# mLSTM stage: short denominator and norm, finished between the next head's products; values projected before queries and keys

## What is computed

```python
qk = silu(causal_depthwise_conv(qk_pre, conv_qk))
...
num = w_inter[..., None] * einsum('bhtd,bhde->bhte', qc, C) + einsum('bhts,bhse->bhte', qk, vc)
den = w_inter * einsum('bhtd,bhd->bht', qc, n) + sum(qk, axis=-1)
h = num / maximum(abs(den), exp(-m_t))[..., None]
...
h = rms_norm(h, head_norm.reshape(MLSTM_HEADS, 1, MLSTM_V_DIM))
h = merge_heads(h).astype(xn.dtype) * sigmoid(og)
```

## Time and profile before

| | |
|---|---|
| median of 3 runs | 2963.53 us (2962.91 to 2967.25) |
| the profiled execution | 2963.58 us |
| its span in the trace | 2961.7 us |
| mean granted TensorE clock | 0.934 of 2.4 GHz |
| TensorE (PE) busy | 2567.9 us, 87% |
| VectorE (DVE) busy | 1241.7 us, 42% |
| ScalarE (ACT) busy | 960.6 us, 32% |
| GpSimd (POOL) busy | 987.9 us, 33% |
| the heads of this stage | from 974.8 to 1236.5 us of the span |

### The profile page before, as it was taken

The page is one execution under the profiler, slowest core; times in us unless marked ns, Lnnn a source line. Parts: engine busy times, 40 slices in busy tenths (PEclk is TensorE's granted clock), DMA queues, the critical chain, the costliest instruction groups (busy, mean ns, idle before and its releaser), DMA issues. The chain is left out here.

```text
span 2961.7 us, 37204 instructions
## 1 busy us (share of the span) xinstructions
PE 2567.9 (87%) x14314; PEld 1852.1 (63%) x14314; DVE 1241.7 (42%) x1578; ACT 960.6 (32%) x1354; POOL 987.9 (33%) x469
## 2 busy tenths in 40 slices
PE   8998898799897899789879999869978698579996
PEld 5776676588775566568658877647577487223334
DVE  5443623566554533362256655341744513411112
ACT  4542422444323233243234442242422321211112
POOL 5222322344375311142233437523111333122321
PEclk9999999899999988899989999979999799799998
DMA  3111222122264111122112226412000121599992
GB/s 120 64 44 57 99 72 84 59 98 99 102 219 147 43 43 42 36 92 100 57 71 99 87 73 237 156 57 92 1 3 25 64 85 57 209 356 346 361 352 99
DMA packets 76275, 333.79 MB, mean 113 GB/s; under 512 B 17114, under 2 KB 21210, under 8 KB 51802
## 3 DMA queue, kind: packets, MB, share of 16 engines
q1 hardware_dynamic: 62336, 313.98, 29.3%
q0 software_dynamic: 13824, 18.19, 1.8%
HBM read 372.67 MB, written 16.78 MB: 131 GB/s over the span
## 5 line engine op out<-in xcount | busy, mean ns | idle before, releaser
L495 POOL TENSOR_TENSOR dense_w_lo<-weights,dense_w_hi 128x1024 fp32r<-128x1024 f32 x84 | 203.3, 2423 | 467.0 <-ACT dense_w_hi L486 467.0
L220 PE MATMUL bank<-dense_s_hi,dense_w_hi 128*128 128x512 f32 x672 | 270.2, 402 | 65.6 <-DVE dense_s_lo L456 35.5
L221 PE MATMUL bank<-dense_s_lo,dense_w_hi 128*128 128x512 f32 x672 | 266.5, 397 | 0.0
L222 PE MATMUL bank<-dense_s_hi,dense_w_lo 128*128 128x512 f32 x672 | 266.5, 397 | 0.0
L486 ACT ACTIVATE dense_w_hi<-weights 128x1024 fp32r<-128x1024 f32 x84 | 88.9, 1058 | 346.2 <-PE bank L222 319.5
L220 PEld LDWEIGHTS bank<-dense_s_hi,dense_w_hi 128*128 128x128 f32 x672 | 129.6, 193 | 104.8 <-POOL dense_w_lo L495 39.3
L1245 DVE TENSOR_TENSOR hidden<-up_y 128x512 f32 x44 | 158.2, 3596 | 64.6 <-ACT up_y L1208 64.0
L222 PE MATMUL bank<-xn_r,weights_r 128*128 128x512 f32 x448 | 177.7, 397 | 0.0
L220 PE MATMUL bank<-xn_r,mix_r 128*128 128x512 f32 x352 | 141.7, 403 | 38.0 <-DVEq L1233 38.0
L1586 DVE SCALAR_TENSOR_TENSOR xn<-mix,xn 128x1024 f32<-128x1024 f32 x64 | 122.3, 1911 | 119.6 <-DMA mix<-in_modulation 106.6
L2743 PE MATMUL bank<-moe_weights,mix 128*64 128x512 f32 x320 | 151.1, 625 | 17.4 <-DMA experts_more_up<-in_experts_up,moe_more_up 17.4
(11 more groups left out here) (634 smaller groups left out, 6134.8 us busy)
## 6 DMA issues: line engine op xcount, KB each, us to landing
weights<-in_w_up SPq DMA_DIRECT2D x44, 1024.0 KB, 4.9
moe_weights<-in_experts_up SPq DMA_DIRECT2D x40, 1024.0 KB
mix<-in_modulation SPq DMA_DIRECT2D x64, 512.0 KB, 4.5
weights<-in_w_xattn SPq DMA_DIRECT2D x24, 1024.0 KB, 5.0
weights<-in_experts_up SPq DMA_DIRECT2D x24, 1024.0 KB
weights<-in_w_down SPq DMA_DIRECT2D x44, 512.0 KB, 3.7
moe_weights<-in_experts_down SPq DMA_DIRECT2D x40, 512.0 KB
weights<-in_w_attn SPq DMA_DIRECT2D x8, 1536.0 KB, 6.3
```

The costliest lines, as they stand in the source:

```text
L220: nc.tensor.matmul(out, left.hi, right.hi, start=first, stop=False)
L221: nc.tensor.matmul(out, left.hi, right.lo, start=False, stop=False)
L222: return nc.tensor.matmul(out, left.lo, right.hi, start=False, stop=last)
L495: nc.gpsimd.tensor_tensor(w[b].lo[:, :], units.rows(b, 0, D, 0, D), w[b].hi[:, :], ALU.subtract).then_inc(w_split, 1)
```

## The change

The denominator is no longer summed into all 128 partitions over 512 columns. It is folded: block b of 128 positions goes into partitions 32b to 32b+31 of bank 6, over 128 columns, by a stationary tile of 32 columns of ones; the row exp(-m) goes into the next 128 columns of the bank in the same way. Absolute value, maximum and reciprocal then work on 128 x 128. Four products with one repeated column of the identity as the stationary tile widen it again to 128 x 512 in bank 7 (`widen`), and ScalarE copies that to `den`. The mean of squares is folded, rooted, inverted and widened in the same way; the scaling reads the widened norm from bank 7.

On TensorE this work no longer stands at the end of the head but between the products of the next one: `widen_den` after the first quarter of the value projection, `head_means` after the third quarter, `widen_head` after the query half of the query/key projection. The last head's three steps stand alone at the end. Values are now projected first, then queries and keys, then the gate, and ScalarE's rounding, GpSimd's rests and VectorE's copies follow that order. SyncE waits for the query/key projection (fourth count), then issues the loads of slots 0 and 1, then waits for the gate.

```diff
+        QK, VALUE, GATE = range(3)
+        ORDER = (VALUE, QK, GATE)
@@ -1277,7 +1281,7 @@
...
-        den = sb("den", [P, T])
+        den, den_short = sb("den", [P, T]), sb("den_short", [P, P])
@@ -1290,16 +1294,14 @@
...
-                for s in range(3):
-                    sp.wait_ge(proj_done, 6 * i - 6 + 2 * s + 2)
+                for s, last in ((QK, 4), (VALUE, 2), (GATE, 6)):
+                    sp.wait_ge(proj_done, 6 * i - 6 + last)
                     units.load(sp, i, s)
@@ -1311,40 +1313,71 @@
...
+            def widen(bank, short):
+                for b in range(TT):
+                    mm = nc.tensor.matmul(bank[:, b * P:(b + 1) * P], g.ident[:, 32 * b:32 * b + 1].broadcast_to([P, P]), short,
+                                          start=True, stop=True)
+                return mm
+
+            def widen_den(i):
+                pe.wait_ge(den_inverted, i + 1)
+                widen(g.bank[7], den_short[:, :]).then_inc(den_wide, 1)
+
+            def head_means(i):
+                for j in range(2):
+                    pe.wait_ge(squared, 2 * i + j + 1)
+                    for b in range(TT):
+                        mm = nc.tensor.matmul(g.bank[6][32 * b:32 * b + 32, 2 * P:3 * P], g.mean_256[:, 0:32],
+                                              sq[:, j, b * P:(b + 1) * P], start=(j == 0), stop=(j == 1))
+                mm.then_inc(mean_done, 1)
+
+            def widen_head(i):
+                pe.wait_ge(head_inverted, i + 1)
+                widen(g.bank[7], g.rstd[:, 0:P]).then_inc(head_wide, 1)
+
             def head(i, first):
-
-                pe.wait_ge(h_ready, 2 * i + 1)
-                for j in range(2):
-                    if j == 0:
-                        pe.wait_ge(w_split[0], i + 1)
-                    for k in range(KT):
-                        c = k * W + j * P
-                        mm = split_products(nc, g.bank[j][:, :], w[0].cut(c, c + P), norm.split[k], k == 0, k == KT - 1)
-                    mm.then_inc(proj_done, 1)
-                pe.wait_ge(w_split[1], i + 1)
-                pe.wait_ge(std_ready, i + 1)
+                pe.wait_ge(w_split[VALUE], i + 1)
+                if not first:
+                    pe.wait_ge(v_ready, 2 * i)
                 for t in range(TT):
                     for k in range(KT):
                         mm = split_products(nc, g.bank[2 + t // 2][:, t % 2 * VD:(t % 2 + 1) * VD], norm.split[k].cut(t * P, (t + 1) * P),
-                                            w[1].cut(k * W, k * W + VD), k == 0, k == KT - 1)
+                                            w[VALUE].cut(k * W, k * W + VD), k == 0, k == KT - 1)
                     if t % 2 == 1:
                         mm.then_inc(proj_done, 1)
+                    if not first:
+                        if t == 0:
+                            widen_den(i - 1)
+                        if t == 2:
+                            head_means(i - 1)
+                pe.wait_ge(w_split[QK], i + 1)
+                if not first:
+                    pe.wait_ge(h_ready, 2 * i)
+                for j in range(2):
+                    for k in range(KT):
+                        c = k * W + j * P
+                        mm = split_products(nc, g.bank[j][:, :], w[QK].cut(c, c + P), norm.split[k], k == 0, k == KT - 1)
+                    mm.then_inc(proj_done, 1)
+                    if not first and j == 0:
+                        widen_head(i - 1)
                 if first:
                     pe.wait_ge(G_ready, 1)
                     for t in range(TT):
                         mm = nc.tensor.transpose(g.bank[4][:, t * H:(t + 1) * H], G[:, t * P:(t + 1) * P], g.ident[0:H, 0:H])
                     mm.then_inc(G_turned, 1)
                     pe.wait_ge(Gc_ready, 1)
...
+                pe.wait_ge(w_split[GATE], i + 1)
...
+                        mm = split_products(nc, g.bank[4 + j][:, :], w[GATE].cut(c, c + P), norm.split[k], k == 0, k == KT - 1)
...
                 pe.wait_ge(qk_ready, 2 * i + 2)
                 pe.wait_ge(rows_ready, 2 * i + 2)
+                if not first:
+                    pe.wait_ge(head_scaled, 2 * i)
@@ -1358,21 +1391,25 @@
...
-                nc.tensor.matmul(g.bank[3][:, :], g.ones[0:H, :], rows[:, 1, :], start=True, stop=True)
                 for kb in range(TT):
                     pe.wait_ge(p_ready, 4 * i + kb + 2)
-                    for j in range(3):
-                        left = v[:, kb, j * P:(j + 1) * P] if j < 2 else g.ones[:, :]
-                        mm = nc.tensor.matmul(g.bank[j][:, kb * P:T], left, probs_T[:, kb, kb * P:T], start=(kb == 0),
-                                              stop=(kb == TT - 1), skip_group_check=True)
+                    for j in range(2):
+                        nc.tensor.matmul(g.bank[j][:, kb * P:T], v[:, kb, j * P:(j + 1) * P], probs_T[:, kb, kb * P:T], start=(kb == 0),
+                                         stop=(kb == TT - 1), skip_group_check=True)
+                for b in range(TT):
+                    nc.tensor.matmul(g.bank[6][32 * b:32 * b + 32, P:2 * P], g.ones[0:H, 0:32], rows[:, 1, b * P:(b + 1) * P],
+                                     start=True, stop=True)
+                for kb in range(TT):
+                    for b in range(kb, TT):
+                        mm = nc.tensor.matmul(g.bank[6][32 * b:32 * b + 32, 0:P], g.ones[:, 0:32], probs_T[:, kb, b * P:(b + 1) * P],
+                                              start=(kb == 0), stop=(kb == b), skip_group_check=True)
                 mm.then_inc(sums_done, 1)
-                for j in range(2):
-                    pe.wait_ge(squared, 2 * i + j + 1)
-                    mm = nc.tensor.matmul(g.bank[3][:, :], g.mean_256[:, :], sq[:, j, :], start=(j == 0), stop=(j == 1))
-                mm.then_inc(mean_done, 1)
             head(0, True)
             with pe.Fori(1, units.n) as i:
                 head(i, False)
+            widen_den(units.n - 1)
+            head_means(units.n - 1)
+            widen_head(units.n - 1)
 
...
 
...
                 for j in range(2):
-                    act.wait_ge(proj_done, 6 * i + j + 1)
+                    act.wait_ge(proj_done, 6 * i + j + 3)
@@ -1412,15 +1449,17 @@
...
                 if later:
-                    for s in range(3):
+                    for s in ORDER:
                         round_weights(i + 1, s)
                 act.wait_ge(sums_done, i + 1)
-                nc.scalar.activation(den[:, :], g.bank[2][:, :], ACT.Abs).then_inc(den_abs, 1)
+                nc.scalar.activation(den_short[:, :], g.bank[6][:, 0:P], ACT.Abs).then_inc(den_abs, 1)
+                act.wait_ge(den_wide, i + 1)
+                nc.scalar.activation(den[:, :], g.bank[7][:, :], ACT.Copy).then_inc(den_copied, 1)
                 for j in range(2):
-                    act.wait_ge(h_ready, 2 * i + j + 2)
+                    act.wait_ge(h_ready, 2 * i + j + 1)
                     nc.scalar.activation(sq[:, j, :], h[:, j, :], ACT.Square).then_inc(squared, 1)
                 act.wait_ge(mean_done, i + 1)
-                nc.scalar.activation(g.std[:, :], g.bank[3][:, :], ACT.Sqrt, bias=g.eps[:, 0:1]).then_inc(std_ready, 1)
+                nc.scalar.activation(g.std[:, 0:P], g.bank[6][:, 2 * P:3 * P], ACT.Sqrt, bias=g.eps[:, 0:1]).then_inc(std_ready, 1)
@@ -1433,12 +1472,12 @@
...
-            rest(0, 0)
+            rest(0, VALUE)
             norm.gpsimd(pool)
-            for s in (1, 2):
+            for s in (QK, GATE):
                 rest(0, s)
             with pool.Fori(1, units.n) as i:
-                for s in range(3):
+                for s in ORDER:
                     rest(i, s)
@@ -1473,13 +1512,17 @@
...
                 for j, row in enumerate((top, em)):
                     nc.vector.tensor_scalar(rows[:, j, :], row[:, :], g.ident[0:H, bass.ds(i, 1)], None,
                                             ALU.mult).then_inc(rows_ready, 1)
+                for j in range(2):
+                    dve.wait_ge(proj_done, 6 * i + 1 + j)
+                    nc.vector.tensor_copy(v[:, 2 * j:2 * j + 2, :], g.bank[2 + j][:, :].rearrange("p (a b) -> p a b", b=VD))\
+                      .then_inc(v_ready, 1)
                 for j in range(2):
                     dve.wait_ge(now_done, 2 * i + j + 1)
...
-                for j in range(2):
-                    dve.wait_ge(proj_done, 6 * i + 3 + j)
-                    nc.vector.tensor_copy(v[:, 2 * j:2 * j + 2, :], g.bank[2 + j][:, :].rearrange("p (a b) -> p a b", b=VD))\
-                      .then_inc(v_ready, 1)
@@ -1502,19 +1541,20 @@
...
                 dve.wait_ge(den_abs, i + 1)
-                own.did(nc.vector.tensor_tensor(den[:, :], den[:, :], g.bank[3][:, :], ALU.max))
+                own.did(nc.vector.tensor_tensor(den_short[:, :], den_short[:, :], g.bank[6][:, P:2 * P], ALU.max))
                 own.wait()
-                own.did(nc.vector.reciprocal(den[:, :], den[:, :]))
-                own.wait()
```

(15 more changed lines are left out.)

10 lines of the change are left out of this document (4 added, 6 removed).

## The result

| | before | after |
|---|---|---|
| median | 2965.39 us (2962.91 to 2967.93, 4 runs) | 2924.06 us (2921.72 to 2928.68, 4 runs) |
| ratio, 95% interval | | 0.9861 (0.9846 to 0.9877) |
| the profiled execution, its span | 2963.58, 2961.7 us | 2924.59, 2922.4 us |
| the stage, first projection to next stage | 261.5 us (975.0 to 1236.5) | 223.9 us (976.9 to 1200.8) |

The change makes the kernel 41 us faster (36 to 46 by the interval). By the two profiled executions it is 39.0 us, of which 37.6 lie in the mLSTM stage. The forecast was a gain of 31.4 us, all of it in the stage, to 2932.2. The measured time lies inside the range of 2921 to 2944, on its fast side, but outside the part that the forecast held likeliest (2927 to 2937): sign and places were right, and several sizes too small.

What follows compares the result with a forecast made beforehand. TensorE, busy 87% of the span, bounds the kernel, so only its idle and slow stretches can be won. 33.8 + 1.1 - 9.9 + 1.9 + 4.5 = 31.4 us off 2963.6 gives 2932.2 us; range 2921 to 2944.

Steps and rivals of the forecast that it cites:

- 1, the gap: From scores' end to the next head's projection: 33.8 us gained over heads 0 to 2, 1.1 in the last.
- 2, the folds: Three folds per head move into the next head's projection and cost 3.3 us there, three times 9.9.
- 3 and 4, chains and order: Each fold's chain hides behind projection products, thinnest cover 1.1 us; values-first weight order costs nothing, slack 1.6 to 3.3 us.
- Rival (c): TensorE waits at the folds for VectorE, gain under 5.9 us, 2958 or more; chance 0.03.
- 5, the warm start: Heads 2 and 3 start their projection at 2.4 GHz without the idle stretch: 1.9 us gained.
- Rival (d): Thin products bring the clock to 1.2 GHz in the projections; slower, at worst 3033 us; chance 0.02.
- The scores: TensorE's scores in each head: stretches at 1.2 GHz kept where they are, no gain or loss.
- 6, the tail: Last head after its sums, nothing to hide it: 12.8 us instead of 17.3 to the last product into mix, gain 4.5.
- Rival (a): Small products do not run side by side and shape changes cost more: 11.6 us lost, to 2943.8; chance 0.18.
- Rival (b): Clock stays up in scores and sums; all four 1.2 GHz stretches gone worth 15 us; 2920 to 2927; chance 0.13.

Runs made afterwards that it cites:

- gate between the scores: Changed kernel with the gate's second half cut up between the score blocks: 2912.5 us in heads 1 to 3, 2903.5 us with head 0 too.
- the kernel that removes the cover: Changed kernel with the denominator's widening ahead of the next head's values instead of behind their first quarter: 2929.9 us, ratio 0.9883.
- the sums sorted: Changed kernel with the ten denominator sums ordered by the 32 partitions they write instead of spread over them: 2925.4 us, ratio 0.9868.
- the gate between all scores: Changed kernel with slices of the gate's second half between the score blocks in every head, head 0 included: 2903.5 us, ratio 0.9798.
- values first alone: Kernel before with only the order changed (values, then queries and keys, then gate), nothing folded or moved: 2965.9 us, ratio 1.0000.
- ten narrow products: Changed kernel with ten more unused 128-column products a head behind the sums, all into the same 32 partitions: 2928.2 us, ratio 0.9881.
- The early table load: Changed kernel with one unused single-column Exp behind the gate's Sigmoid, pulling the Exp table's load ahead of the scores: 2914.4 us, ratio 0.9831.

## Why the prediction came out as it did

The stage gave 37.6 us where the sum said 31.4. The mechanism was right, and the terms below were off in size. Step by step:

**1, the gap: 42.2 us instead of 34.9,** the largest miss. From scores' end to next head 8.07 us three times (forecast 10.3, 9.3, 9.4), the last head's sums 5.85 (8.4). Two terms were mis-sized. Folded products and shape changes: 1.36 us against 1.85 + 0.45, 0.94 per head, 3.8 us. I had named nearly the right price as a bound (the busiest 32 partitions alone, 1.1) and then chosen the issue rate of eight later records, where twenty records here lay 0.05 us apart. The changes of shape, priced at 0.45, are inside the 1.36: the ten sums are followed by the next full product without a gap (1.01 us from start to start). And the half rate: I kept the stretches in their places and charged 3.7, 2.7, 2.8 and 1.75 us; the low part of the sums was 4.6 us three times and none in the last head, so 2.3, 2.3, 2.3 and 0, together 4.0 us less. That part is luck: nothing in the forecast said that the stretches would shift, and in other kernels of this series they lie otherwise. At full clock the block is 5.77 us, as in every head with the gate between the scores; the value sums in it are 4.4, forecast 4.3.

**2, the folds: 2.8 us per head instead of 3.3.** Means 0.57 instead of 1.35, by the same mistake. The two widenings take 0.81 each, priced 0.88, so the repeated column of the identity costs nothing extra. The other 0.6 us of the 2.8, where 0.2 was put for waits, stand at no fold, and where they arise is open. 1.4 us gained in three heads.

**3 and 4, chains and order: right.** Denominator ready 1.7 us after the sums (1030.26 against 1028.57), asked at 2.9; no wait of TensorE at a fold or at a new weight until the last head. Rival (c) has nothing for it, and the kernel that removes the cover shows what it would have been.

**5, the warm start: right.** All projections with folds take 36.4 us, 2.8 more than the warm 33.65. Rival (d), the slower side, falls with them: here the thin products between dense ones left the clock at 1.00.

**The scores: a term that I had set to zero, 1.7 us lost.** They take 9.0, 10.1, 10.1 and 6.8 us against 9.2, 8.7, 9.5 and 6.9. In heads 1 and 2 the clock falls at 4.5 us from their start, so 5.6 us of them run at half rate, where before it was 1.2 and 4.3.

**6, the tail: 13.6 us to the last product into mix instead of 12.8** (13.9 to the next stage), gain 3.7 instead of 4.5.

The timelines of TensorE and ScalarE in the tail:

```profile
1188.56 1.74 PE L1318 MATMUL bank<-mlstm_den_short,ident 128*128 128x128 f32 x8 [1.68 <-DVE mlstm_den_short L1546]
...
1195.64 2.07 PE L1318 MATMUL bank<-stds,ident 128*128 128x128 f32 x8 [2.01 <-DVE stds L1551]
```

```profile
1192.94 1.28 ACT L1462 ACT_TABLE_LOAD   x1
1194.24 0.37 ACT L1462 ACTIVATE stds<-bank,eps 128x128 f32<-128x128 f32 x1
```

The clock fell to 1.2 GHz at 1189.0, in the first widening, which so took 1.8 us to its reader instead of 0.98. The 1.68 us of idling before it don't explain that: they are the same in all eleven runs with a folded tail. In after and its repetition the clock fell inside the widening; in the nine others it fell 1.6 us or more after the widening's start, which then ran at full rate. Why is open. The second widening took 2.2 to its reader instead of 1.85. The table load lies on the path as forecast, 1.30 us from its start to the square root. The Trainium skill, ScalarE: Activation LUTs, section What ACT_TABLE_LOAD costs, adds a drain of 1.38 us to the load; here too the trace shows none.

Together: 31.4 + 7.3 + 1.4 - 1.7 - 0.8 = 37.6.

**What lies outside the stage.** Its length is 2700.2 us before and 2698.5 after, but 2691.8 with the sums sorted, 2694.1 with the gate between all scores and 2704.6 with values first alone, whose other stages are the same code. The time at 1.2 GHz outside the stage doesn't explain this: it is 324 and 325 us before and after, 317 and 311 in the first two, but 315 with ten narrow products, whose other stages take 2698.0. What decides it stays open. A few microseconds of any comparison of this kernel are of this kind.

Rival (a) falls by the prices above. Rival (b) named the time (2920 to 2927), but not the cause: its stretches did not vanish, three of four stayed, and of the 15 us that it put on them 1.7 came (30.6 - 27.2, halved). Of what was gained beyond the forecast, 5.2 us are in prices (3.8 in the gap, 1.4 in the folds), and 4.0 less 1.7 in where the clock was low.

## What to carry to other kernels

Where a chain of small steps on other engines ends each pass of a loop, finish it between the products of the next pass: the move alone shortened the stage by 31.8 us, the shorter vectors alone by 12.3, both together by 37.6. Price thin products by the busiest group of partitions that they write, and spread them over the groups. And try to fill sparse stretches of TensorE with dense work that is due anyway: a gate block laid between the scores, with no work saved, took another 16.5 us out of the stage. The early table load, a single instruction, took out 8.7 on its own, so try the cheap edit first.

## What the hardware showed that was not expected

- Stretches at 1.2 GHz within scores and sums lasted 3.4, 6.8 or 10.2 us in every kernel here that had any; small edits changed which of them a head had, or removed one. An edit whose block cost 1 us more then read as 4 in the stage (the sorted sums), and only the rows of the block itself could decide.
- Products of 128 columns into the same 32 partitions cost 0.23 us each, as much as into 128 (0.226). Into different 32 partitions they run side by side, four spreads in 0.35 us, also where they belong to different sums (records of L1407 between those of L1404).
- The clock fell with no idle time shown before it in the last head of before (at 1210.8, TensorE busy since the scores began at 1202.5) and in head 1 with the early table, with TensorE busy all through the scores. It stayed at 2.4 GHz in the scores with dense products between them, but for head 0 of the first such kernel, which had a wait of 1.88 us.
